# Who weights and adds the rows of the modulation beside the first FFN: GpSimd before, VectorE after

## The reference, cut to what matters

```
mod   = silu(cond) @ ada_w + ada_b                  # 9 sections of 1024; two conditions: context, latent
h     = rmsnorm(x, w0) * (1 + mod[1]) + mod[0]
x    += 0.5 * mod[2] * (silu(h @ A) * (h @ B)) @ D   # first FFN, 2816 hidden
h     = rmsnorm(x, w1) * (1 + mod[4]) + mod[3]
x    += mod[5] * token_mixer(h)
h     = rmsnorm(x, w2) * (1 + mod[7]) + mod[6]
x    += 0.5 * mod[8] * second_ffn(h)
y     = rmsnorm(x, final_norm)
```

## Time and profile before

| | |
|---|---|
| median of 3 runs | 3318.6 us (3316.32 to 3326.79) |
| the profiled execution's own time | 3318.82 us |
| its span, first to last instruction | 3317.0 us |
| TensorE matmuls busy | 2978.8 us, 90% |
| VectorE busy | 1503.2 us, 45% |
| ScalarE busy | 770.0 us, 23% |
| GpSimd busy | 877.9 us, 26% |
| mean granted TensorE clock | 0.950 of full speed |

### The profile page before, as it was taken

The page is one execution under the profiler, slowest core; times in us unless marked ns, Lnnn a source line. Parts: engine busy times, 40 slices in busy tenths (PEclk is TensorE's granted clock), DMA queues, the critical chain, the costliest instruction groups (busy, mean ns, idle before and its releaser), DMA issues. The chain is left out here.

```text
span 3317.0 us, 56526 instructions
## 1 busy us (share of the span) xinstructions
PE 2978.8 (90%) x23320; PEld 2816.9 (85%) x23320; DVE 1503.2 (45%) x2475; ACT 770.0 (23%) x1286; POOL 877.9 (26%) x870
## 2 busy tenths in 40 slices
PE   7999987679798799999599996979979999999998
PEld 4999987679797798999488873769969999999996
DVE  4543432333334436342487847334563343334334
ACT  4111101111012323443033333321141111111112
POOL 4821888888201201222112113012240000000000
PEclk8999988889899899999699998989999999999999
DMA  6211222221112143344544312242111111111111
GB/s 242 79 52 60 80 59 78 70 77 55 39 38 90 47 139 117 140 150 159 161 99 97 88 48 78 82 157 75 48 35 56 50 44 39 38 38 38 38 38 63
DMA packets 187989, 263.88 MB, mean 80 GB/s; under 512 B 80816, under 2 KB 136112, under 8 KB 186288
## 3 DMA queue, kind: packets, MB, share of 16 engines
q1 hardware_dynamic: 178608, 236.35, 22.0%
q0 software_dynamic: 9216, 25.18, 2.7%
HBM read 206.35 MB, written 55.12 MB: 79 GB/s over the span
## 5 line engine op out<-in xcount | busy, mean ns | idle before, releaser
L660 DVE SCALAR_TENSOR_TENSOR x<-bank,gate,x 128x128 f32<-128x128 f32 (+1 forms) x832 | 411.3, 515 | 210.0 <-PE bank L774 209.5
L824 DVE TENSOR_TENSOR g_ffn<-act_out_ffn,bank 128x384 f32<-128x384 f32 x132 | 73.1, 554 | 759.8 <-ACT act_out_ffn L821 759.8
L821 ACT ACTIVATE act_out_ffn<-bank 128x384 f32<-128x384 f32 x132 | 64.9, 492 | 1403.7 <-PE bank L759 1403.7
L759 PE MATMUL bank<-h_hi_ffn,wlo_a_ffn 128*128 128x384 f32 x1056 | 365.2, 346 | 19.7 <-DVE g_ffn L824 8.2
L759 PE MATMUL bank<-h_lo_ffn,whi_a_ffn 128*128 128x384 f32 x1056 | 362.5, 343 | 0.0
L759 PE MATMUL bank<-h_hi_ffn,whi_a_ffn 128*128 128x384 f32 x1056 | 362.4, 343 | 0.0
L759 PE MATMUL bank<-h_hi_ffn,whi_b_ffn 128*128 128x384 f32 x1056 | 355.3, 336 | 0.0
L759 PE MATMUL bank<-h_hi_ffn,wlo_b_ffn 128*128 128x384 f32 x1056 | 355.3, 336 | 0.0
L759 PE MATMUL bank<-h_lo_ffn,whi_b_ffn 128*128 128x384 f32 x1056 | 355.3, 336 | 0.0
L774 PE MATMUL bank<-g_hi_ffn,wlo_d_ffn 128*128 128x384 f32 x1056 | 353.0, 334 | 2.4 <-DVE g_lo_ffn L682 2.4
L774 PE MATMUL bank<-g_lo_ffn,whi_d_ffn 128*128 128x384 f32 x1056 | 352.8, 334 | 0.0
(11 more groups left out here) (252 smaller groups left out, 5475.9 us busy)
## 6 DMA issues: line engine op xcount, KB each, us to landing
ada_beside_ffn<-in_ada_w POOLq DMA_DIRECT2D x192, 128.0 KB, 2.6
raw_a_ffn<-in_ffn_w SPq DMA_DIRECT2D x44, 512.0 KB, 4.7
raw_b_ffn<-in_ffn_w SPq DMA_DIRECT2D x44, 512.0 KB, 5.3
raw_d_ffn<-in_ffn_w SPq DMA_DIRECT2D x44, 512.0 KB, 3.6
raw_in<-in_w_in SPq DMA_DIRECT2D x35, 512.0 KB, 5.2
mix<-row_out SPq DMA_DIRECT2D x23, 576.0 KB, 3.1
sc_ar<-streams SPq DMA_DIRECT2D x36, 256.0 KB, 3.5
sc_bkv<-streams SPq DMA_DIRECT2D x36, 256.0 KB, 4.2
```

Source lines behind the costliest of these rows:

```text
L660: ins = nc.vector.scalar_tensor_tensor(xs, kit.banks[4 + d % 4][:, a:b], kit.gate[:, gate, d, cond:cond + 1], xs, ALU.mult, ALU.add)
L759: mm = nc.tensor.matmul(kit.banks[2 * slot + j][:, 0:CH], w[q][:, par, cols], v[:, k, toks], start=(k == 0 and m == 0), stop=(k == ku - 1 ...
L821: return self.nc.scalar.activation(out, a, ACT.Silu)
L824: self.nc.vector.tensor_tensor(g32, act_out, b, ALU.mult).then_inc(g32_ready, 1)
```

## The change

Five things change.

- **The units.** VectorE makes them (`make_unit`): for each row tile and condition one instruction on 128 x 256, the first a multiplication, the others `raw * silu + acc`, 16 in all. Each waits on `unit_step` until the one two places before it is finished. GpSimd waits until a unit is done and then issues the four transfers of the next, two row tiles (256 KB) each, into one set of eight buffers. There are two accumulators per condition in place of four.
- **Where they stand.** Three units per pair over pairs 2 to 9, in place of four over pairs 3 to 8. On VectorE, the third unit of a pair stands after step (0,1), the first and the second of the next pair after steps (1,1) and (1,2). TensorE sums two after `up` (0,1) and one after `up` (1,0). VectorE's and TensorE's loops are cut accordingly: pair 1 and, on VectorE, pair 9, on TensorE pair 10, are written out.
- **The opening.** TensorE turns section 0 before it makes the rows of section 1; VectorE normalises three tiles and adds section 0 before it splits the first weights; the rows have three places instead of two.
- **Three buffers** for `x_normed` and `h_full` in all three norms. In the opening `low(m)` stands ahead of the normalisation of tile m + 3; in `Norm` the subtraction follows two tiles behind.
- **The reciprocal** in `Norm` is made in place in `inv`, and stands ahead of the last two subtractions of the chunk before.

```diff
+DEEP, LAG = 3, 2
...
     def vector(self, dve, split_weights):            # Norm
         for m in range(NC * KT):
             c, k = divmod(m, KT)
             if k == 0:
-                if c:
-                    low(m - 1)
                 dve.wait_ge(self.rms_ready, c + 1)
-                nc.vector.reciprocal(self.inv[:, c % 2], self.rms[:]).then_inc(self.inv_ready, 1)
+                nc.vector.reciprocal(self.inv[:, c % 2], self.inv[:, c % 2]).then_inc(self.inv_ready, 1)
                 dve.wait_ge(self.inv_ready, c + 1)
-            if m >= 2:
-                dve.wait_ge(self.hi_ready, m - 1)
-                dve.wait_ge(self.full_ready, m - 1)
+            if m >= DEEP:
+                dve.wait_ge(self.hi_ready, m - DEEP + 1)
+                dve.wait_ge(self.full_ready, m - DEEP + 1)
...
-            if k:
-                low(m - 1)
-        low(NC * KT - 1)
+            if m >= LAG:
+                low(m - LAG)
+        for m in range(NC * KT - LAG, NC * KT):
+            low(m)
...
-    SUMS = {(0, 2): (0, 1), (1, 0): (2, 3)}
+    SUMS = {(0, 1): (0, 1), (1, 0): (2,)}
+    MADE = {(0, 1): (0, 2), (1, 1): (1, 0), (1, 2): (1, 1)}
...
         self.rows_of(pe, 0, (0, 1))
-        self.rows_of(pe, 1, (2, 3))
         pe.wait_ge(self.S["select_loaded"], 16)
         pe.wait_ge(self.rms_ready, 3)
         self.turn(pe, 0)
+        self.rows_of(pe, 1, (2, 3))
         self.turn(pe, 1)
...
     def sections(self, pool):
         pool.wait_ge(self.h_ready, NC * KT)
+        pool.wait_ge(self.S["mod_turned"], 3)
+        for u in range(self.UNITS):
+            i, q = divmod(12 + u, 4)
+            if u:
+                pool.wait_ge(self.S["unit_step"], 16 * u)
+            for g in range(4):
+                pool.dma_start(self.raw[:, 2 * g:2 * g + 2],
+                               self.kit.dram["ada_w"][i, g, :, :, q * self.QW:(q + 1) * self.QW]).then_inc(self.unit_loaded, 16)
...
+    def make_unit(self, dve, i, j):
+        S = self.S
+        dve.wait_ge(self.unit_loaded, i * 192 + (64 * j - 320))
+        if not (isinstance(i, int) and i == 2 and j < 2):
+            dve.wait_ge(S["unit_turned"], i * 3 + (j - 7))
+        for k in range(KT):
+            for cond in range(2):
+                acc, by = self.acc[:, j % 2, cond], self.silu[:, k, cond:cond + 1]
+                if k == 0:
+                    ins = self.nc.vector.tensor_scalar(acc, self.raw[:, k], by, None, ALU.mult)
+                else:
+                    dve.wait_ge(S["unit_step"], i * 48 + (16 * j + 2 * k + cond - 97))
+                    ins = self.nc.vector.scalar_tensor_tensor(acc, self.raw[:, k], by, acc, ALU.mult, ALU.add)
+                ins.then_inc(S["unit_step"], 1)
...
         self.squares(1, dve, 0)                        # Opening.vector
         for c in range(NC):
             dve.wait_ge(self.rms_ready, c + 1)
             nc.vector.reciprocal(self.inv[:, c], self.inv[:, c]).then_inc(self.inv_ready, 1)
+        for m in range(DEEP):
+            normed(m)
         self.add_section(dve, 0)
+        split_weights()
         self.add_section(dve, 1)
         self.scales(0, S["scale_ready"])
-        split_weights()
         for m in range(NC * KT):
+            low(m)
+            if m + DEEP < NC * KT:
+                normed(m + DEEP)
```

More of the change, by code:

```diff
@@ L101, in __init__ @@
         self.sq = buf("square", [P, 3, 2, CH])
-        self.rms = buf("rms", [P, CH])
         self.inv = buf("inv_rms", [P, 2, CH])
-        self.xn = buf("x_normed", [P, 2, CH])
-        self.full = buf("h_full", [P, 2, CH])
-        self.scratch_width = 13 * CH
+        xn, full = buf("x_normed", [P, DEEP, CH]), buf("h_full", [P, DEEP, CH])
+        self.xn, self.full = ([v[:, i] for i in range(DEEP)] for v in (xn, full))
+        self.scratch_width = (8 + 2 * DEEP) * CH
         self.sq_ready = [kit.sem(f"sq_ready_{o}_n{n}") for o in ("act", "dve", "pool")]
@@ L238, in __init__ @@
         self.inv = buf("inv_rms", [P, NC, CH])
-        self.xn = buf("x_normed", [P, 2, CH])
-        self.full = buf("h_full", [P, 2, CH])
-        self.rows = self.sq[:].rearrange("p o b t -> p (o b t)")[:, 0:4 * 512].rearrange("p (s h x) -> p s h x", s=2, h=2)
+        xn, full = buf("x_normed", [P, 2, CH]), buf("h_full", [P, 2, CH])
+        past = self.sq[:].rearrange("p o b t -> p (o b t)")
+        third = past[:, 0:D].rearrange("p (h x) -> p h x", h=2)
+        self.rows = [rows[:, 0], rows[:, 1], third]
+        self.xn = [xn[:, 0], xn[:, 1], past[:, D:D + CH]]
+        self.full = [full[:, 0], full[:, 1], past[:, D + CH:D + 2 * CH]]
         self.sq_ready = [kit.sem(f"sq_ready_{o}_n0") for o in ("act", "dve", "pool")]
@@ L694, in _, with pair @@
                 first_weights()
-            def pair(i, early=False, last=False, beside=False):
+            def pair(i, early=False, last=False, beside=False, made=()):
                 for par in range(2):
@@ L700, in pair @@
                         if beside and (par, c) == (1, 0):
-                            opening.add_section(dve, i)
+                            opening.add_units(dve, i)
+                        if (par, c) in made:
+                            ahead, j = opening.MADE[par, c]
+                            opening.make_unit(dve, i + ahead, j)
             pair(0, early=True)
             if opening:
-                with dve.Fori(1, 3) as i:
-                    pair(i)
-                with dve.Fori(3, 9) as i:
-                    pair(i, beside=True)
+                a, b = opening.PAIRS
+                pair(1, made=((1, 1), (1, 2)))
+                with dve.Fori(a, b - 1) as i:
+                    pair(i, beside=True, made=opening.MADE)
+                pair(b - 1, beside=True, made=((0, 1),))
                 opening.finish(dve)
-                with dve.Fori(9, pairs - 1) as i:
-                    pair(i)
             else:
@@ L793, in _ @@
             if opening:
-                with pe.Fori(1, 3) as i:
-                    pair(i)
-                with pe.Fori(3, 9) as i:
+                pair(1)
+                with pe.Fori(*opening.PAIRS) as i:
                     pair(i, beside=True)
-                with pe.Fori(9, pairs) as i:
-                    pair(i)
+                pair(pairs - 1)
             else:
```

135 lines of the change are left out of this document (50 added, 85 removed).

## The result

| | median | lowest to highest |
|---|---|---|
| before | 3322.7 us (4 runs) | 3316.3 to 3329.0 |
| after | 3171.5 us (4 runs) | 3168.9 to 3180.7 |

The ratio is 0.955, 95% interval 0.9521 to 0.9579: 151 us less by the medians. In a second series of runs it was 0.9548 (0.9524 to 0.9573), 3171.55 us against 3317.93, 146 us less. The forecast was 3168 us. The profiled execution of the changed kernel took 3180.7 us, 9 us above the median of its series, so differences read from its trace add up to less than the medians say.

A forecast was written before the change was run, and what follows sets the result against it. It took GpSimd, making units too slowly for TensorE's sums, to bound the first FFN's pairs. Units 131.5 + opening 4 + mixer's norm 7 + second FFN's norm 8 = 150.5 us, off 3318.8: 3168 us, range 3153 to 3194.

The forecast's parts named there:

- The units: First FFN's pairs: units on VectorE lie beside matmuls, so the excess of pairs 4 to 8 goes, 131.5 us within 2.
- the sums: TensorE's summing of units in the first FFN: 24 before and after, so 0, with 2 us either way.
- The instruction: One VectorE multiply-add of 128 x 256 in a unit: 477 ns; sixteen take 7.0 us, lower bound 6.5.
- The room: VectorE's time for a unit before TensorE waits: 9.0 us after step (1,1), 10.0 after step (1,2).
- The loads: GpSimd's four 256 KB transfers per unit: issued in 2.3 us, landed in 5.6, inside the 8.5 that cost nothing.
- The opening: Start of first FFN: first `h_full` 1.0 us sooner, then a faster norm with three buffers; 4 us (2 to 4.5).
- The mixer's norm: Norm ahead of the mixer: chunk 2 complete 6.3 us sooner, plus 0.7 for slow matmuls; 7 us.
- I take 1.2 us a tile: Chunks 1 and 2 of a norm with three buffers: 1.2 us per tile instead of 1.41, lower bound 1.05.
- the lock: The skill's rule that two-input VectorE and GpSimd SBUF operations never overlap: 2.15 us a tile; rejected against the trace's 1.41.
- The late first up: Mixer: the reciprocal ahead of two subtractions delays TensorE's first `up` by 2.5 us, hidden by its wait for chunk 1.
- The second FFN's norm: Norm ahead of the second FFN: third `up` 6 us sooner, plus 2 us of slow matmuls; 3 at 1.41 a tile.
- the norms give nothing: Rival, chance 0.17: VectorE and GpSimd slow each other, 1.41 us a tile stays, or late chunk 0 costs more; 3180 us.

The follow-up runs named there:

- units_alone: The kernel before with the units on VectorE and their loads as in the change; norms, opening and buffers as before; 3180.14 us, ratio 0.9581.
- double: The changed kernel with VectorE making a second multiply-add, 128 x 176, ahead of each of a unit's 14; 3194.84 us.
- aligned: The changed kernel with buffer `select` widened from 2 to 16 words, so first-FFN buffers behind it lie at multiples of 64 bytes; 3174.40 us.
- norms_alone: The kernel before with the change's norms, three buffers, reciprocal and opening; units stay on GpSimd at their old places; 3309.20 us, ratio 0.9967.

## Why the prediction was right, and where not

The mechanism of the large term was right, the sum nearly so: 150.5 us forecast; 151.2 and 146.4 measured. But the small terms failed, and the errors went in two directions.

- **The units, 131.5 us within 2: right** in the traces, where the first FFN's end came 133.4 us sooner (units_alone). The difference is the sums, which I had put at 0: 24 units cost (78.07 - 75.86)/3 = 0.74 us each, where the earlier trace rows had 0.8, so 17.7 us instead of 19.6. By the medians they gave 137.8.
- **The instruction, 477 ns: right** (479; one starts every 0.40 us behind the last). The 16 take 6.16 us; I took 7.0 and gave 6.5 as the lower bound, so I had allowed for too little overlap of neighbours (0.08 us each). L1877's 1002 ns was indeed the odd one. Nothing hung on it: the `g` waits for ScalarE, not for the unit.
- **The room, 9.0 and 10.0 us: right in the sum**, by *double*.
- **The loads: right.** Four issues take 2.9 us, not 2.3 (0.724 us each for 256 KB), a transfer 3.5 us in the median. GpSimd waited 587 us for VectorE, and VectorE never for a transfer.
- **The opening, 4 us: 1.9 and 0.4.** So much sooner stood the third up in the two traces of the changed kernel (82.5 and 84.0 for 84.3), and 3.5 where the clock was at its upper level (80.8 in aligned). The first `h_full` was to come at 45.8. In three traces of kernels with this opening it came at 45.7 to 45.9, in six others at 46.9 to 48.8. The same 32 matmuls for the rows of section 1 took 3.64 us at a clock of 1.00 (37.58 in the trace of aligned) and 5.34 or 6.56 us where the clock of 36 to 44 us was 0.79 or 0.57 (the two traces of the changed kernel). The new order lets TensorE stand idle for 1.1 us for the select transfer just ahead of them and makes ScalarE's split wait for them; I had priced neither. The pace was the second miss: the 24 tiles took 33.9 us where they took 35.9, so 2 us of my 3.4.
- **The mixer's norm, 7 us: failed.** The step that failed is "I take 1.2 us a tile": it was 1.37. I set the bound at VectorE's and GpSimd's own durations and rejected the lock since 1.13 + 1.02 exceeds 1.41. But GpSimd's 1.13, read while VectorE worked beside it, already held the time of standing still. (VectorE's 1.02 is two undisturbed instructions, 0.47 + 0.55.) With undisturbed durations (0.66 for GpSimd, beside the reciprocal, and two starts at 0.47) a lock over whole instructions gives 1.60 us, still more than 1.41. So that lock is contradicted either way; the wrong step was to conclude that the two don't bind each other. The 1.41 us were also well above the 0.94 of VectorE and the 0.66 of GpSimd, and what the runs show is in between: 0.94 and half of the 0.87 us in which VectorE yields, 1.37. With the clock at its upper level at the stage's start, the new norm gave 2.8 us at the third up (norms_alone). In the changed kernel the low clock there, which I hadn't foreseen, took it back: the third up came 0.3 us later than before in one trace and 0.9 sooner in the other. The late first up, 2.5 us by the reciprocal, was right (2.7 in norms_alone), and was hidden as said.
- **The second FFN's norm, 8 us: failed by the same step.** It gave 3.0 at the third up and 3.7 at the fourth, 2.5 and 3.1 in the second trace; its bound "at 1.41 us a tile it is 3 in all" was the better value.

So the rival "the norms give nothing", to which I gave 0.17, had the truer mechanism, VectorE and GpSimd slowing each other, though its 3180 us was too slow by 9. That units_alone also took 3180 us is a coincidence: the rival's sum has 7 us of small terms in it, units_alone has none. That the forecast hit within 4 us is luck in part: the small terms were too large by 10 us, and the units gave 2 us more in the traces and 6 in the medians, where no run shows why.

## What to carry to other kernels

When a wait stands out in the list, take its excess over an undisturbed period of the same loop: it held the slow matmuls behind the waits, 16.6 us of 131.5, that the waits themselves don't show. Don't test whether two engines hold each other up with durations taken while they run side by side; take one of each from a stretch where the other is still, look for an instruction that is alternately short and long, and when the full exclusion doesn't fit, ask how much of it does before you drop it. Where VectorE and GpSimd take turns, a deeper buffer buys little, and a third engine buys more where it has room: moving half of GpSimd's tiles to ScalarE cut the opening's norm by a fifth, and brought the mixer's third up only 1.7 to 3.0 us forward, since ScalarE was full in chunk 0.

## What the runs showed of the hardware that I had not expected

- GpSimd's scaling of 128 x 384 takes 0.66 us beside a VectorE reciprocal, and 1.05 and 1.73 us in turn beside VectorE's subtractions and multiplications of SBUF data; VectorE's instruction in turn grows from 0.55 to 0.86 us, by 0.8 ns per column that GpSimd moves (0.31 us for 384, 0.15 for 192). One-input multiplications by a constant are held up likewise (0.35 to 0.67), reciprocals not seen to be.
- At the start of the mixer's stage, behind a wait of 2.5 us, the granted clock was 0.53 to 0.76 over 7 us in twelve traces with the units on VectorE and 1.00 in two with them on GpSimd. The length of the work ahead, some 840 and 200 us, doesn't explain it: behind a like wait after some 115 us it was 0.76 in both kernels.
- The level of the clock in the opening differs from one execution of the same code to the next (0.57 and 0.79 from 36 to 44 us in the changed kernel's two traces, 1.00 in that of aligned, with the same order of work). The 32 matmuls on the path there took 6.56, 5.34 and 3.64 us, up to 3 us of difference.
- In the first FFN matmuls of one kind start 173.3 or 176 to 177 ns apart in the mean, and which of them do changes with where the buffers lie and with what ran before. The cause is open.
